# Delta-rule scan: decay factors from loaded rows of cumulative sums instead of TensorE differences

## The reference

```python
def gated_delta_chunked(q, k, v, g, beta, s0):
    gc = jnp.cumsum(g, axis=-1)
    incl = jnp.tril(jnp.ones((DN_CHUNK, DN_CHUNK), bool))
    strict = jnp.tril(jnp.ones((DN_CHUNK, DN_CHUNK), bool), -1)
    diff = gc[..., :, None] - gc[..., None, :]
    decay = jnp.where(incl, jnp.exp(jnp.where(incl, diff, 0.0)), 0.0)
    kb = k * beta[..., None]
    m = jnp.where(strict, jnp.einsum('bhncd,bhnsd->bhncs', kb, k) * decay, 0.0)
    a = m + jnp.eye(DN_CHUNK, dtype=m.dtype)
    u = triangular_solve(a, v * beta[..., None]);  w = triangular_solve(a, kb * jnp.exp(gc)[..., None])
    attn = jnp.where(incl, jnp.einsum('bhncd,bhnsd->bhncs', q, k) * decay, 0.0)
    ...
    def step(s, inp):
        v_new = ui - jnp.einsum('bhck,bhkv->bhcv', wi, s)
        o = jnp.einsum('bhck,bhkv->bhcv', qd, s) + jnp.einsum('bhcs,bhsv->bhcv', ai, v_new)
        s = s * jnp.exp(gl)[..., None, None] + jnp.einsum('bhck,bhcv->bhkv', kd, v_new)
        return s, o
```

## Time and profile before

| | |
|---|---|
| median of 3 runs | 3645.32 us (3641.82 to 3646.91) |
| the profiled execution's own time | 3644.86 us |
| its span in the trace | 3643.1 us |
| mean granted clock of TensorE | 0.971 |
| TensorE, VectorE, ScalarE, GpSimd busy | 95%, 48%, 27%, 23% of the span |
| HBM traffic | 144 GB/s over the span |

### The profile page before, as it was taken

The page is one execution under the profiler, slowest core; times in us unless marked ns, Lnnn a source line. Parts: engine busy times, 40 slices in busy tenths (PEclk is TensorE's granted clock), DMA queues, the critical chain, the costliest instruction groups (busy, mean ns, idle before and its releaser), DMA issues. The chain is left out here.

```text
span 3643.1 us, 41402 instructions
## 1 busy us (share of the span) xinstructions
PE 3450.2 (95%) x15660; PEld 2184.6 (60%) x15660; DVE 1749.0 (48%) x2642; ACT 988.1 (27%) x1973; POOL 836.3 (23%) x824
## 2 busy tenths in 40 slices
PE   6999999799999996899999999999879999999998
PEld 2445444799974444444444444445567878788786
DVE  4454554455557533452223222234366666666666
ACT  4365566244445110311111111122201111111113
POOL 1022222466537000201111111123221121212211
PEclk9999999899999998999999999999869999999999
DMA  8222322666656116821111221044326656666566
GB/s 296 73 76 81 98 81 67 197 214 208 196 170 193 61 47 219 274 97 56 58 58 47 95 70 58 26 157 142 136 94 232 220 183 209 203 204 215 179 209 254
DMA packets 365358, 524.08 MB, mean 144 GB/s; under 512 B 60764, under 2 KB 236415, under 8 KB 364969
## 3 DMA queue, kind: packets, MB, share of 16 engines
q1 hardware_dynamic: 341844, 462.72, 38.0%
q0 software_dynamic: 12096, 43.84, 4.6%
q10 hardware_dynamic: 11221, 14.87, 1.1%
HBM read 411.51 MB, written 111.97 MB: 144 GB/s over the span
## 5 line engine op out<-in xcount | busy, mean ns | idle before, releaser
L2832 POOL TENSOR_TENSOR mg<-mg,sg_m 128x512 f32<-128x512 f32 x64 | 98.1, 1533 | 778.1 <-DVE sg_m L2713 778.1
L3719 PE MATMUL bank<-xeT,raw_e 128*128 128x128 f32 x2304 | 267.9, 275 | 0.8 <-ACT xeT L3563 0.8
L3719 PEld LDWEIGHTS bank<-xeT,raw_e 128*128 128x128 f32 x2304 | 263.6, 192 | 8.3 <-issue 8.3
L2619 PE MATMUL bank<-hT,raw_w 128*128 128x512 f32 x576 | 261.8, 597 | 5.2 <-PEq L2423 5.2
L957 POOL TENSOR_SCALAR sg<-tmp 128x512 f32<-128x512 f32 (+1 forms) x76 | 113.5, 1494 | 427.7 <-DVE tmp L1025 367.6
L2619 PEld LDWEIGHTS bank<-hT,raw_w 128*128 128x128 f32 x576 | 110.4, 192 | 144.2 <-issue 144.2
L3719 PE MATMUL bank<-T_e,U 128*128 128x128 f32 x1536 | 176.7, 275 | 0.0
L3719 PEld LDWEIGHTS bank<-T_e,U 128*128 128x128 f32 x1536 | 174.1, 192 | 0.0
L2619 PE MATMUL bank<-zT,S 128*128 128x512 f32 x384 | 172.6, 592 | 0.0
L685 PE MATMUL bank<-T_d,S_d 128*128 128x512 f32 x384 | 171.5, 593 | 0.0
L2713 DVE TENSOR_TENSOR sg_m<-sg_m,bank 128x512 f32<-128x512 f32 x64 | 43.9, 686 | 228.0 <-PE bank L2631 228.0
(11 more groups left out here) (544 smaller groups left out, 6983.0 us busy)
## 6 DMA issues: line engine op xcount, KB each, us to landing
raw_e<-in_exp_w_gate SPq DMA_DIRECT2D x16, 3072.0 KB, 16.4
raw_e<-in_exp_w_up SPq DMA_DIRECT2D x16, 3072.0 KB, 12.9
raw_e<-in_exp_w_down SPq DMA_DIRECT2D x16, 3072.0 KB, 10.3
raw_w<-in_w_in SPq DMA_DIRECT2D x24, 1024.0 KB, 5.8
raw_d<-in_w_in SPq DMA_DIRECT2D x16, 1024.0 KB, 5.9
raw_h<-in_w_in SPq DMA_DIRECT2D x12, 1024.0 KB, 5.3
x0T<-in_ada_w SPq DMA_DIRECT2D x44, 256.0 KB, 3.3
raw_h<-kT_d SPq DMA_DIRECT2D x36, 256.0 KB, 5.4
```

The lines of the kernel that those rows point to most:

```text
L2619: mm = pe.matmul(bank[:, :], lhs[:, k, :], rhs[:, k, :], start=first and k == 0, stop=k == 3, skip_group_check=not first)
L2832: pool.tensor_tensor(mg[:, i, :], mg[:, i, :], sg[:, i, :], ALU.add).then_inc(add_ok[i], 1)
L3719: mm = pe.matmul(bank[:, f * P:(f + 1) * P], lhs[:, k, f * P:(f + 1) * P], rhs[:, k, :], start=fresh and k == 0, stop=k == 3, skip_group_c ...
```

## The change

In the projection stage, one block after the sums, four matmuls put the cumulative sums of all chunks out as rows (one row for each chunk, direction and head), ScalarE copies them, and a DMA stores them to a new tensor `cr_d` in memory. ScalarE also keeps the negated sums as columns (`ncum`). In the scan, SP loads for each chunk and direction the four rows of sums to all 128 partitions (256 KB, a broadcast). DVE adds to them, one scalar_tensor_tensor a head, the negated sum of the partition's own token (a column) and a table `off` (0 where the decay is kept, -1e30 elsewhere). ScalarE takes one exponential a direction into the attention buffer. `differences` on PE, `decays` and `masked` on GpSimd go away. The places in each engine's order and SP's queue are in the diff.

```diff
@@ projection, SP
+                        if Q == SUMS_AT + 2:
+                            sp.wait_ge(sums_ok, 9)
+                            sp.dma_start(cr_d.rearrange("i r t -> r i t"), crs[:, :, :]).then_inc(img_ok, 16)
@@ projection, PE
+                    def gate_rows_of_sums():
+                        pe.wait_ge(c11_ok, SUMS_AT + 1)
...
+                        for i in range(4):
+                            c0 = i % 2 * NCH // 2
+                            last = pe.matmul(Y[0:NCH * 4, i * P:(i + 1) * P], g_all[:, c0:c0 + NCH // 2, :].rearrange("p c g -> p (c g)"), tri[:, UI + i // 2, :], start=True, stop=True)
...
+                        if Q == SUMS_AT + 1:
+                            gate_rows_of_sums()
...
+                        if Q == SUMS_AT + 1:
+                            pe.wait_ge(sums_ok, 9)
@@ projection, ScalarE
+                        for d in range(2):
+                            act.activation(ncum[:, :, d * 4:d * 4 + 4], Y[:, d * 80:(d + 1) * 80].rearrange("p (c h) -> p c h", h=4),
+                                           ACT.Copy, scale=-1.0).then_inc(sums_ok, 1)
+
+                    def gate_rows_of_sums():
+                        act.wait_ge(sums_mm, 2)
+                        act.activation(gT_all[:, 0, :], Y[0:NCH * 4, :], ACT.Copy).then_inc(sums_ok, 1)
@@ scan, buffers
+            cum_rows = lambda f, d: (CR[:, d], R[:, d], V[:, d], O[:, 1, d])[f if f < AHEAD else 0]
@@ scan, SP
+                    def load_sums(f):
+                        for d in range(2):
+                            if f >= AHEAD:
+                                sp.wait_ge(Em_ok, nth(0 if f == AHEAD else f - 1, d))
+                            sp.dma_start(cum_rows(f, d), sums_of(f, d).rearrange("h t -> (h t)").unsqueeze(0).to_broadcast([P, HEADS * P])).then_inc(cum_sem(f), 16)
...
+                    sp.wait_ge(img_ok, 80)
+                    load_sums(0)
                     load_front(0)
+                    load_sums(1)
                     load_front(1)
...
-                    load_front(2)
+                    load_sums(2)
+                    load_sums(3)
                     store_gram(0)
                     store_gram(1)
                     load_blocks(0)
+                    load_front(2)
                     load_front(3)
                     load_keys(0)
                     load_values(0)
                     store_gram(2)
-                    sp.wait_ge(img_ok, 64)
                     store_blocks(0)
                     load_inverse(0)
                     load_inverse(1)
                     store_gram(3)
                     load_blocks(1)
+                    load_sums(4)
                     load_front(4)
                     for s in range(STEPS):
...
                         if s + AHEAD + 1 < STEPS:
+                            load_sums(s + AHEAD + 1)
                             load_front(s + AHEAD + 1)
@@ scan, PE
-                    def differences(f):
...
-                        if ahead:
-                            differences(f)
                         corrected(s, 0)
                         corrected(s, 1)
@@ scan, ScalarE
-                        act.activation(E[:, :, :].rearrange("p h c -> p (h c)"), PS[front_bank(f, 0)][:, :], ACT.Exp).then_inc(E_ok, 1)
+                    def decay(f, d):
+                        act.wait_ge(cm_ok, nth(f, d))
+                        if f >= DEEP:
+                            act.wait_ge(out_mm, nth(f - DEEP, d))
+                        act.activation(attn(f, d), cum_rows(f, d), ACT.Exp).then_inc(Em_ok, 1)
...
                         f, m = s + AHEAD, s + 1
+                        if f < STEPS:
+                            for d in range(2):
+                                decay(f, d)
                         if m < STEPS:
                             other_halves(m, 0)
                         finished(s)
                         scaled(s, 0)
                         scaled(s, 1)
-                        if f < STEPS:
-                            decay(f)
@@ scan, GpSimd: decays and masked removed everywhere
@@ scan, DVE
+                    dve.tensor_scalar(off[:, :, :], tri[:, UI:UI + 2, :], -1.0, 1e30, ALU.add, ALU.mult).then_inc(neg_ok, 1)
...
+                    def masked(f, d):
+                        dve.wait_ge(cum_sem(f), cum_loads(f))
+                        dve.wait_ge(neg_ok, 1)
+                        for h in heads:
+                            last = dve.scalar_tensor_tensor(cum_rows(f, d)[:, h, :], cum_rows(f, d)[:, h, :], column(ncum, f, d, h), off[:, d, :], ALU.add, ALU.add)
+                        last.then_inc(cm_ok, 1)
...
+                    for f in range(2):
+                        for d in range(2):
+                            masked(f, d)
                     for f in range(2):
                         for d in range(2):
                             gram(f, d)
...
-                    front(2)
+                    for f in range(2, AHEAD):
+                        for d in range(2):
+                            masked(f, d)
                     solve(dve, 0, 0)
                     solve(dve, 0, 1)
+                    front(2)
                     front(AHEAD - 1)
+                    for d in range(2):
+                        masked(AHEAD, d)
                     for l in range(NL):
                         crossed(0, l)
                         joined(0, l)
...
                         rest(s, 0)
                         rest(s, 1)
+                        if f + 1 < STEPS:
+                            for d in range(2):
+                                masked(f + 1, d)
                         if merging:
                             crossed(m, 0)
```

More of the change, by code:

```diff
@@ L140, in build @@
     mg_d = scr("mg_d", (KD, P, SEQ))
+    cr_d = scr("cr_d", (4, NCH * 4, P))
     mod_d = scr("mod_d", (1, 4 * D))
@@ L717, in gate_sums @@
                                              g_all[:, :, d * 4:d * 4 + 4], start=True, stop=True)
+                        last.then_inc(sums_mm, 1)
+                    def gate_rows_of_sums():
+                        pe.wait_ge(c11_ok, SUMS_AT + 1)
+                        if SUMS_AT in ctx_no:
+                            pe.wait_ge(cx_ok, ctx_no[SUMS_AT] + 1)
+                        for i in range(4):
+                            c0 = i % 2 * NCH // 2
+                            last = pe.matmul(Y[0:NCH * 4, i * P:(i + 1) * P], g_all[:, c0:c0 + NCH // 2, :].rearrange("p c g -> p (c g)"), tri[:, UI + i // 2, :], start=True, stop=True)
                         last.then_inc(sums_mm, 1)
@@ L1157, in build @@
             at_bufs = [AT4[:, n] for n in range(4)] + [AT6[:, n] for n in range(6)]
-            gS, TTF, S, R, V, O = big("gS", 2), big("TTF", 2), big("S", 2), big("R", 2), big("V", 2), sbt(st, "O", [P, 2, 2, HEADS, P])
-            E, N2, E1, Tq, TTm = [sbt(st, n, [P, HEADS, P]) for n in ("E", "N2", "E1", "Tq", "TTm")]
+            CR, TTF, S, R, V, O = big("CR", 2), big("TTF", 2), big("S", 2), big("R", 2), big("V", 2), sbt(st, "O", [P, 2, 2, HEADS, P])
+            N2, E1, Tq, TTm = [sbt(st, n, [P, HEADS, P]) for n in ("N2", "E1", "Tq", "TTm")]
+            off = sbt(st, "off", [P, 2, P])
             Tb = sbt(st, "Tb", [P, 2, 2, 256])
@@ L1243, in load_front, with sums_of @@
                             sp.dma_start(qF[:, f % 2, d], chunked(qT_d, f, d)).then_inc(ldf[f % 2], 16)
+                    def sums_of(f, d):
+                        half, c = divmod(chunk(f, d), NCH // 2)
+                        return cr_d[2 * d + half, c * 8 + d * 4:c * 8 + d * 4 + 4]
+                    def load_sums(f):
[3 more added lines that the diff above has]
+                            sp.dma_start(cum_rows(f, d), sums_of(f, d).rearrange("h t -> (h t)").unsqueeze(0).to_broadcast([P, HEADS * P])).then_inc(cum_sem(f), 16)
                     def load_keys(s):
@@ L1564, in _ @@
                 def _(pool):
[L1565 to L1572, removed]
-                        pool.wait_ge(E_ok, f + 1)
-                        pool.tensor_tensor(attn(f, d), E[:, :, :], mask4(tri[:, UI + d, :]), ALU.mult).then_inc(Em_ok, 1)
                     def decayed_keys(s):
@@ L1583, in decayed_state @@
                         pool.tensor_tensor(S[:, d], S[:, d], per_token(etot, s, d), ALU.mult).then_inc(sx_ok, 1)
-                    decays(0)
-                    decays(1)
-                    for f in range(2):
-                        for d in range(2):
-                            masked(f, d)
-                    decays(2)
-                    for d in range(2):
-                        masked(2, d)
-                    decays(3)
                     pool.wait_ge(inv, INV)
-                    for d in range(2):
-                        masked(3, d)
                     decayed_keys(0)
-                    decays(4)
                     solve(pool, 1, 0)
@@ L1603, in _ @@
                             decayed_state(s, d)
-                        if f < STEPS:
```

(4 more changed lines are left out.)

25 lines of the change are left out of this document (11 added, 14 removed).

## The result

The changed kernel takes **3729.07 us** (median of 4 runs, 3724.26 to 3736.56) against 3644.39 us for the kernel before (4 runs, 3641.82 to 3646.91): ratio 1.0232, 95% interval 1.0215 to 1.0249. The forecast was 3682 us (3650 to 3706): the sign holds, and the size is missed by 47 us. It is the fastest of the four, 4.8 us under their median.

The account below looks back on a forecast made before the run. PE was taken as the bound, busy 95% of the span and without idle time in the loop. 3644.9 + 18.2 (loop, 43.2 - 25.0) + 15.4 (clock) + 3 (opening) + 0.9 (projection) = 3682.4, forecast 3682 us, range 3650 to 3706.

Parts of the forecast that it names:

- Differences off PE, −25.0: Scan loop: PE loses the differences, 1.79 us a step, 25.0 us gained over 14 loop steps.
- Stalls, 43.2: Loop steps 1 to 12: PE waits before the outer merge, 1.9 us in even and 5.3 in odd steps, 43.2 us.
- the broadcasts' form: Loop loads of sums: a broadcast read could be slower than a plain one, 0 to 4 us, taken as 0.
- Clock, 15.4: Loop: PE's granted clock falls behind five odd-step gaps, 3.1 us each, 15.4 us; bounds 0 and 18.6.
- the even ones not: Loop: only odd-step stalls exceed 4.74 us, so even-step gaps were given no clock cost.
- Masks beside GpSimd: Loop masks on DVE: colliding with GpSimd could cost 1.2 us a pair, 14 us in all; taken as 0.
- Projection stage, +0.9: Projection stage: four more matmuls for the rows of sums on a dense PE add 0.9 us.
- The opening, +3: Scan opening: PE's first outer merge moves from 689.61 to 692.5, +3 us; bounds -2 and +6.
- the solve starts some 5 us earlier: Scan opening: DVE's solve no longer stands behind front(2), so it starts some 5 us earlier.
- Sums in time (3621): Rival: loop masks end before 8.6 us in every step, PE stays dense, about 3621 us; chance 10%.
- No fall of the clock: Rival: PE stalls in the loop, but odd gaps stay too short to drop the clock, 3667 us; chance 22%.
- Slow masks: Rival: stalls, plus masks colliding with GpSimd and slow broadcasts, 14 + 4 us more, 3700 us; chance 10%.

Follow-up runs that it names:

- e5: The changed kernel with two buffers of sums for each direction, loaded in the loop a step before their masks: 3642.01 us, ratio 0.9982.
- e4: The changed kernel with a semaphore for each direction's sums in the loop, so each mask waits only for its own load: 3717.89 us, ratio 1.0192.
- e3: The changed kernel with the loads of sums reading 128 different plain rows (queries) in place of one broadcast row: 3723.79 us, ratio 1.0203.
- e6: e5 with its opening changed: semaphores for each of the first four chunks, front(2) ahead of the solve, loads reordered: 3633.62 us, ratio 0.9959.
- e8: e6 with the sums of chunks 1 and 2 loaded behind their front loads and chunk 3 masked behind the solve: 3633.13 us, ratio 0.9955.
- e1: The changed kernel with the loop's load of the sums moved in SP's queue to right behind the keys: 3677.36 us, ratio 1.0078.

## Why the prediction was right or wrong

*Differences off PE, −25.0: right.* The dense step of e5 is 1.79 us shorter, and so is step 13 of the change, which masks nothing (20.29 us).

*Stalls, 43.2: the mechanism right, the size 19.4 too small (62.6).* The failed step is "I take the landing of the first front load of each step as the landing of the first sums". On average the sums are issued where that load was foreseen (4.8 us into odd steps and 3.1 into even ones, against 4.9 and 3.2), but the masks start at 13.3 and 10.1, not at 11.7 and 8.3. Three things were wrong in it. First, the step's loads grow by the 512 KB of the sums themselves, in engines that are full, and the sums come out with the whole batch. Second, "the second direction's sums arrive while the first are being masked" took no notice of the code: `cum_loads` counts both loads, so the first mask waits for the second load (e4: stalls 7.5 us shorter without that, 11.2 us of time). Third, the broadcasts' form, for which 0 to 4 us had been allowed: stalls 5.3 us shorter without it (e3). Beside these, masks in even steps take 2.5 to 2.8 us against 2.16, 3 us in all. The first item was not run by itself; if e3 and e4 add up, some 7 of the 19.4 us are left for it, an estimate.

*Clock, 15.4: right in kind, too small (24.0), and two errors in it partly cancelled.* The rest of the step (11.04 us at full clock) takes 12.5 to 13.9 us in 11 of 12 steps, 20.5 us in all, and another 3.5 us are spread over the steps, 0.2 ahead of the gap and 0.1 behind it. The step that failed is "the even ones not": five of the six even gaps, 3.05 to 4.74 us, cost 10.1 us. The price was off the other way: an odd gap was taken at 3.1 us from a row elsewhere and cost 1.4 to 2.1, 10.4 us for all six. The Trainium skill, "TensorE: Matmul & The Clock Gate", section "Why this matters for your kernels", warns of idle gaps between bursts of matmuls. The trace agrees for the kind: 11 of the 12 gaps here were followed by the lower clock, one of 3.31 us was not.

*Masks beside GpSimd: a cost near the bound, its place hidden.* In e5, where the masks fall beside GpSimd's operations, the 96 operations of the twelve steps take 339 to 1132 ns each, 406 at the median. A pair of directions takes 3.2 us on average against 2.19 alone: 1.0 us more, where the bound was 1.2, but in five odd steps 1.6 (3.75 us). That agrees with the Trainium skill, "GPSIMD Engine Reference", section "Specifications". It costs nothing there, since DVE's hole holds it.

*Projection stage, +0.9: right.* The scan's first operation is at 645.02 against 644.0.

*The opening, +3: wrong by about 14.* Step 1 starts 16.5 us later; the forecast's own terms make that 3 + 0.9 − 1.8 (step 0 without its differences) = 2.1. The sentence that failed is "the solve starts some 5 us earlier": it starts 2.1 us later. The masks of chunks 0 to 3 stand ahead of it on DVE, 8.4 us of work that the forecast of the opening did not count. The solve's first operation before, DVE, and the block stores, SP:

```profile
671.21 0.28 DVE L1215 COPY Tb<-gm 128x256 f32<-128x256 f32 x1
```

```profile
679.40 1.92 SPq L1279 DMA_DIRECT2D ti_d<-Tb  x4
```

The kernel after, DVE, then SP, then PE:

```profile
654.98 2.19 DVE L1634 SCALAR_TENSOR_TENSOR CR<-CR,ncum,off 128x128 f32<-128x128 f32 x8 [8.46 <-DMA R<-cr_d]
...
669.07 2.18 DVE L1634 SCALAR_TENSOR_TENSOR V<-V,ncum,off 128x128 f32<-128x128 f32 x8
671.17 2.19 DVE L1634 SCALAR_TENSOR_TENSOR O<-O,ncum,off 128x128 f32<-128x128 f32 x8
673.27 0.29 DVE L1247 COPY Tb<-gm 128x256 f32<-128x256 f32 x1
...
701.94 2.85 DVE L1634 SCALAR_TENSOR_TENSOR CR<-CR,ncum,off 128x128 f32<-128x128 f32 x8 [11.88 <-DMA CR<-cr_d]
```

```profile
685.31 2.25 SPq L1322 DMA_DIRECT2D ti_d<-Tb  x4
...
696.24 0.96 SPq L1286 DMA_DIRECT2D CR<-cr_d  x2
```

```profile
705.44 2.08 PE L1395 MATMUL bank<-E,TTm 128*128 128x128 f32 x8 [9.74 <-DVE E L1677]
```

The very first masks wait for the sums of chunk 1 (one semaphore for two chunks); with a semaphore for each chunk (e6) the first Gram product on DVE starts 2.4 us earlier. The solve is late, `front(2)` behind it holds up the block stores, as foreseen, and these are issued at 685.31, where 679.40 was before. So the first inner merge comes 6.9 us later. Then PE waits 9.74 us for `crossed` behind `masked(4)`, which ends at 704.8, not 692: its sums were issued at 696.24, not 687.2, since SP's order in front had slipped too. The prediction had worked this stretch from positions in SP's queue, without following the new links of DVE's chain.

*The rivals.* Sums in time (3621) is what e5 makes of the loop; in the change as it stands no mask of steps 1 to 12 started before 9.2. "No fall of the clock" is refuted by the windows. Slow masks came true only in part, and that case reached just 3700. The profiled execution is 42 us above the sum: 19.4 from the stalls, 8.6 from the clock, 14.4 from the opening, less 0.5 elsewhere. The loop's 28 us alone would have carried the sum past 3706; the opening's 14.4 alone would not.

**A version that beats both** is e6 or e8: the change with its sums a step ahead and the opening mended in part, 0.4% under the kernel before.

## What to carry to other kernels

A transfer issued into full DMA queues should be given the landing of its whole batch, its own bytes included, not that of the neighbour whose place it takes (here 1.6 to 1.8 us a step too early); and a wait's count must be read in the code for what else it takes in. An input that replaces a computation should be asked for one step of the loop earlier than its use: here two more buffers took back the whole loss of 2.3% (e5, 0.2% under the kernel before). Where an engine that was dense gets gaps, the clock's price is to be added to each gap of a few microseconds, here 1.4 to 2.9 us behind 11 of 12 gaps, and a stage's opening is to be followed link by link as carefully as its loop, since there every added wait counts once in full.

## What had not been expected of the hardware

- A gap of 2.04 us on PE was followed by 1.6 us lost to the lower clock, and one of 2.52 us in the same kernel by none (e1). Three gaps of 2.2 to 2.6 us in e3 lost 1.6 us each.
- One issue of two 256 KB broadcasts occupied SP's queue for 6.25 us (e6; 6.39 in the change), where others take 0.8 to 2.9 us. It did so behind fourteen other transfers issued in the 7 us before, and not where four stood in front (e8: 0.91 us). Plain loads at the same place took 5.71 us (e3), so it is not the broadcast.
- Stores of 32 KB took 4.2 us to land behind 2 MB of loads from the same queue (e8), so that work finished 3.3 us earlier gave 0.3 us.
